# Delta heads: squares taken in the units' rounds, tail loads and residual loads moved, accumulator banks taken singly

## The reference

```
# layer 0
q, k, v, z, g, beta = project(h), with a short convolution and silu on q, k, v
o = delta_forward + delta_backward                      # [768, 8 heads, 128]
o = rmsnorm(o) * norm_g * silu(z)                       # mean of squares over the 128 of a head
y = o @ dn_w_out
x = layernorm(ALPHA * x + gt1 * y) ;  x = layernorm(ALPHA * x + gt2 * swiglu(x))   # context rows too
# layer 1
y = subln(softmax(q0 k0) v - lambda * softmax(q1 k1) v) @ da_w_out                 # 512 rows only
x = layernorm(ALPHA * x + gt1 * y) ;  x = layernorm(ALPHA * x + gt2 * swiglu(x))
```

## Time and profile before

| | us |
|---|---|
| median of 3 runs | 4401.18 (4395.31 to 4401.67) |
| profiled execution | 4397.03, its span 4395.1 |
| PE busy | 3927.8 (89% of the span) |
| DVE, ACT, POOL busy | 2124.2, 1593.9, 589.2 |
| PE idle, longest single wait in an output projection | 22.3 |

### The profile page before, as it was taken

How to read it: one execution, slowest core, us unless ns; L and a number is a source line. 1 busy time by engine, 2 the same in 40 slices (tenths; PEclk the granted TensorE clock), 3 DMA queues, 4 the chain that set the end, 5 groups by cost and what they waited for, 6 DMA issues and landing times.

```text
span 4395.1 us, 67095 instructions
## 1 busy us (share of the span) xinstructions
PE 3927.8 (89%) x28034; PEld 3252.3 (74%) x28034; DVE 2124.2 (48%) x3091; ACT 1593.9 (36%) x2560; POOL 589.2 (13%) x692
## 2 busy tenths in 40 slices
PE   6978897877999987987799988899999998899999
PEld 4866686765888775755688776677788787677887
DVE  3545454646221353266423566454655437645564
ACT  3332333333111223154222333543434335544333
POOL 0044303632000001001200000200120003100220
PEclk9988898888999999999899986899999999899999
DMA  4243433121221121102133230031233230222222
GB/s 154 76 150 123 137 94 114 34 95 48 68 68 58 53 69 67 58 10 88 56 98 96 82 77 20 22 125 49 87 98 102 86 106 31 89 96 68 96 96 86
DMA packets 248532, 355.04 MB, mean 81 GB/s; under 512 B 9299, under 2 KB 158502, under 8 KB 247846
## 3 DMA queue, kind: packets, MB, share of 16 engines
q1 hardware_dynamic: 233840, 300.49, 21.2%
q0 software_dynamic: 13840, 50.11, 3.6%
q10 hardware_dynamic: 550, 0.17, 0.0%
HBM read 336.50 MB, written 14.24 MB: 80 GB/s over the span
## 4 chain that ended last, share of the span: by engine, by line
PE 76%; DVE 11%; ACT 7%; POOL 2%; issue 2%; DMA 1%; ACTq 0%; DVEq 0%; SPq 0%; POOLq 0%
PE psum L233 20%; PE psum L235 20%; PE psum L234 20%; PE psum L230 13%; ACT arena L341 3%; PE psum L239 3%; DVE arena L264 3%; DVE arena L274 2%; POOL arena L379 2%; DVE rx L335 1%; ACT arena L345 1%; DVE arena L278 1%; DVE rw L264 1%; ACT rw L345 1%; DVE arena L270 1%
## 5 line engine op out<-in xcount | busy, mean ns | idle before, releaser
L233 PE MATMUL psum<-rx,rw 128*128 128x512 f32 (+2 forms) x2768 | 1024.9, 370 | 47.9 <-DVE rx L335 30.4
L234 PE MATMUL psum<-rx,rw 128*128 128x512 f32 (+2 forms) x2768 | 1009.3, 365 | 0.0
L235 PE MATMUL psum<-rx,rw 128*128 128x512 f32 (+2 forms) x2768 | 1008.1, 364 | 0.0
L230 PE MATMUL psum<-arena 32*32 32x32 f32 (+10 forms) x13078 | 834.2, 260 | 177.5 <-ACT arena L345 59.7
L264 DVE TENSOR_TENSOR rw<-arena,rw 128x2048 fp32r<-128x2048 f32 (+2 forms) x239 | 535.4, 2240 | 898.7 <-ACT rw L345 893.9
L230 PEld LDWEIGHTS psum<-arena 32*32 32x32 f32 (+5 forms) x13078 | 652.6, 144 | 340.7 <-issue 101.6
L345 ACT ACTIVATE rw<-arena 128x2048 fp32r<-128x2048 f32 (+2 forms) x239 | 448.1, 1875 | 847.1 <-PE psum L235 824.6
L233 PE MATMUL psum<-rw,rx 128*128 128x512 f32 (+1 forms) x1720 | 679.7, 395 | 79.7 <-DVE arena L264 40.9
L234 PE MATMUL psum<-rw,rx 128*128 128x512 f32 (+1 forms) x1720 | 673.2, 391 | 0.0
L235 PE MATMUL psum<-rw,rx 128*128 128x512 f32 (+1 forms) x1720 | 673.1, 391 | 0.0
L233 PEld LDWEIGHTS psum<-rx,rw 128*128 128x128 f32 (+1 forms) x2768 | 529.8, 191 | 146.1 <-DVE rx L335 42.7
(11 more groups left out here) (71 smaller groups left out, 2055.0 us busy)
## 6 DMA issues: line engine op xcount, KB each, us to landing
arena<-in_ffn_w_up SPq DMA_DIRECT2D x66, 1024.0 KB, 5.2
arena<-in_ada_w SPq DMA_DIRECT2D x48, 1024.0 KB, 5.2
arena<-in_ffn_w_down SPq DMA_DIRECT2D x40, 1024.0 KB, 5.0
arena<-in_ffn_w_gate SPq DMA_DIRECT2D x22, 1024.0 KB, 5.3
arena<-in_dn_w_in SPq DMA_DIRECT2D x32, 512.0 KB, 5.3
arena<-in_xa_w_kv SPq DMA_DIRECT2D x16, 1024.0 KB, 5.0
arena<-in_hgrn_w_in SPq DMA_DIRECT2D x16, 1024.0 KB, 5.5
arena<-in_da_w_in SPq DMA_DIRECT2D x12, 1024.0 KB, 5.1
```

The source lines that it names most:

```text
L230: return self.e.matmul(out, l, r, start=start, stop=stop)
L233: self.e.matmul(out, l[0], r[0], start=start, stop=False)
L234: self.e.matmul(out, l[0], r[1], start=False, stop=False)
L235: return self.e.matmul(out, l[1], r[0], start=False, stop=stop)
```

## The change

Five things.

1. The 24 squares of a group (`act_tail_square`, one for each chunk and head) are no longer made at the tail. ACT makes them during the units, one at the end of a round: the one of chunk of unit n and head h4 from round 5n + 25 + h4 on, what is left after the last round (`rest`), ahead of the meeting. Then mean, root and reciprocal are made once for all 24 columns. The transposes and gates of the tail come one round (group 0) or one step k (group 1) earlier.
2. `pool_tail_loads` stands before the meeting instead of behind it, waits for `qS` of unit 11, and for group 1 its places are those of k^ (`WK`) and of its transpose (`WK + 2 * HB`) instead of the units' memory. As `tail_first` now lies in `K.X`, the load of `x` and `ctx` (`x1`) waits for `o_lo` of head 3 and stands behind the gate rows and layer norm rows; the gate rows go to `UB`.
3. In layer 1 the rows come back into the place of v (`da_rows`, `WK + 10240`), right after the attention's last product; POOL's gain and bias (`res2`) follow that load at once, and `dve_out` reads them there (`old`) and writes `K.X`.
4. `pe_out` takes each bank just before its first matmul, not all `nt` at the start of a half.
5. The remaining loads of POOL's list in layer 1 (gate rows, layer norm rows, constants) stand behind the `res2` work.

```
@@ pe_out
     for c, (h, k0, kn) in enumerate(out_chunks(Kn)):
         if k0 == 0:
-            bs = [p.bank(tag, t, h) for t in range(nt)]
+            bs = {}
...
+            if t not in bs:
+                bs[t] = p.bank(tag, t, h)
@@ dve_out
-                    v.stt(xs, xs, ALPHA, tmp, MUL, ADD).then_inc(*v.sig((tag + "_x", t, h)))
+                    was = xs if old is None else old[:, t, h * 512:(h + 1) * 512]
+                    v.stt(xs, was, ALPHA, tmp, MUL, ADD).then_inc(*v.sig((tag + "_x", t, h)))
@@ pe_dn_proj
-        if hg and 2 <= r < 6:
-            pe_tail(p, K, 0, r - 2)
+        if hg and 1 <= r < 5:
+            pe_tail(p, K, 0, r - 1)
@@ act_dn_proj
-        if hg and r < 4:
-            act_tail_square(a, K, 0, r)
-            a.root(tail_sums(K, r), ("tail", 0, r))
+        if hg and r == 0:
+            act_tail_root(a, K, 0)
@@ dve_dn_proj
+        if hg and r == 0:
+            dve_tail_root(v, K, 0)
         if hg and r < 4:
-            dve_tail_mean(v, K, 0, r)
             dve_tail_norm(v, K, 0, r)
...
+SQUARES = [(n, h4) for n in range(12) if second_visit(n) for h4 in range(4)]
+def act_tail_square(a, K, hg, n, h4):
+    c = UNITS[n][1]
+    a.wait_ge(*K.at("o", hg, n))
+    a.act(K.mem(CO + 2016, 128), o_sum(K)[:, c, h4, :], ACT.Square, accum_out=tail_sums(K)[:, c * 4 + h4:c * 4 + h4 + 1]
+          ).then_inc(*a.sig(("tail_ss", hg)))
+def act_square_rounds(a, K, hg):
+    left = list(SQUARES)
+    def each(rnd):
+        if left and rnd >= 5 * left[0][0] + 25 + left[0][1]:
+            act_tail_square(a, K, hg, *left.pop(0))
+    def rest():
+        while left:
+            act_tail_square(a, K, hg, *left.pop(0))
+    return each, rest
...
+def dve_tail_root(v, K, hg):
+    ss, rq = tail_sums(K), norm_mem(K)[0][:, 0:24]
+    v.wait_ge(*K.at("tail_ss", hg))
+    v.tt(ss, ss, rq, MUL).then_inc(*v.sig())
     v.tt(ss, ss, rq, MUL).then_inc(*v.sig())
+    v.rstd(ss, 128.0, 1e-6, ("tail", hg))
+    v.tt(ss, ss, rq, MUL).then_inc(*v.sig())
...
 def act_last_tail(a, K):
+    act_tail_root(a, K, 1)
+    a.wait_ge(*K.at("o_ld"))
     for s in range(6):
         if s < 4:
-            act_tail_square(a, K, 1, s)
-            a.wait_ge(*K.at("o_ld"))
             act_tail_hi(a, K, s, tail_first(K, s))
-            a.root(tail_sums(K, s), ("tail", 1, s))
...
@@ pool_tail_loads
-    g.own()
     if hg:
         g.load(("o_ld",), [(tail_first(K, h4), K.o_s[h4]) for h4 in range(4)])
+    g.wait_ge(*K.at("qS", hg, 11))
     g.load(("z_ld", hg), [(tail_gate(K, hg, h4), K.z_s[hg * 4 + h4]) for h4 in range(4)])
...
@@ act_program
-        staggered([act_unit(a, K, hg, n) for n in range(12)], side)
+        each, rest = act_square_rounds(a, K, hg)
+        staggered([act_unit(a, K, hg, n) for n in range(12)], side, each)
+        rest()
@@ pool_program
+        pool_tail_loads(g, K, hg)
         g.meet(f"delta{hg}")
-        pool_tail_loads(g, K, hg)
-    x, c = (K.I[n][0].rearrange("(t p) n -> p t n", p=128) for n in ("x", "ctx"))
-    g.load(("x1",), [(K.X[:, 0:4, :], x), (K.X[:, 4:6, :], c)])
-    pool_gates(g, K, ("gate_rows", 0, 0), 0, 0, WK + 6144, 2)
+    pool_gates(g, K, ("gate_rows", 0, 0), 0, 0, UB, 2)
     pool_ln_cols(g, K)
     pool_ln_rows(g, K, ("ln_rows", 1), CO + C_ONE, "ln1", 0)
+    g.wait_ge(*K.at("o_lo", 3))
+    g.load(("x1",), [(K.X[:, 0:4, :], x), (K.X[:, 4:6, :], c)])
...
-    g.wait_ge(*K.at("daT", 7))
-    g.load(("x2",), [(K.mem(WK, 4096), K.x_s)])
+    g.load(("x2",), [(da_rows(K), K.x_s.rearrange("p (t n) -> p t n", n=1024))])
+    pool_affine(g, K, "res2", range(4), ("ln_rows", 2), WK + 7168, lambda t: ("x2",), da_rows(K))
...
-    pool_affine(g, K, "res2", range(4), ("ln_rows", 2), WK + 7168, lambda t: ("x2",))
```

More of the change, by code:

```diff
@@ L816, in act_out, with dve_out @@
             between[c]()
-def dve_out(v, K, tag, Kn, nt, src=None, gate=None, between=(), after=None, made=0, have=None, begun=0):
+def dve_out(v, K, tag, Kn, nt, src=None, gate=None, between=(), after=None, made=0, have=None, begun=0,
+            old=None):
     between, end = dict(between), len(out_chunks(Kn))
@@ L962, in pool_ln_rows, with pool_affine @@
     g.load(key, [(row, K.I[f"{which}_{n}"][i].partition_broadcast(128)) for row, n in zip(pair_of(K, base), "gb")])
-def pool_affine(g, K, tag, tiles, rows, base, ready):
+def pool_affine(g, K, tag, tiles, rows, base, ready, X):
     gain, bias = pair_of(K, base)
@@ L970, in pool_affine @@
         g.wait_ge(*K.at(*ready(t)))
-        g.tt(K.X[:, t, :], K.X[:, t, :], gain, MUL).then_inc(*g.sig())
-        g.tt(K.X[:, t, :], K.X[:, t, :], bias, ADD).then_inc(*g.sig((tag, t)))
+        g.tt(X[:, t, :], X[:, t, :], gain, MUL).then_inc(*g.sig())
+        g.tt(X[:, t, :], X[:, t, :], bias, ADD).then_inc(*g.sig((tag, t)))
 def swiglu_order(nt):
@@ L1397, in dve_dn_proj @@
             v.tile()
-        if hg and 2 <= r < 6:
-            dve_tail_gate(v, K, 0, r - 2)
+        if hg and 1 <= r < 5:
+            dve_tail_gate(v, K, 0, r - 1)
 def dve_norms(v, K, hg):
@@ L1488, in prior, with staggered @@
     return (hg, n - 2) if n >= 2 else None
-def staggered(units, side):
+def staggered(units, side, each=None):
     units, live, rnd = list(units), [], 0
@@ L1502, in staggered @@
             next(side, None)
+        if each:
+            each(rnd)
 def pe_unit(p, K, hg, n):
@@ L1801, in tail_gate, with tail_sums @@
 def tail_gate(K, hg, h4):
-    return K.mem(WK + h4 * HB + 3 * 768, 768) if hg == 0 else K.mem(UB + h4 * 768, 768)
+    return K.mem(WK + h4 * HB + 3 * 768, 768) if hg == 0 else K.mem(WK + 2 * HB + h4 * 768, 768)
 def tail_first(K, h4):
-    return K.mem(UB + HB + h4 * 768, 768)
-def tail_sums(K, h4):
-    return K.small(316, 24)[:, h4 * 6:h4 * 6 + 6]
+    return K.mem(WK + h4 * 768, 768)
+def tail_sums(K):
+    return K.small(316, 24)
 def tail_rows(K, h4):
     return o_sum(K)[:, :, h4, :]
+SQUARES = [(n, h4) for n in range(12) if second_visit(n) for h4 in range(4)]
[13 more added lines that the diff above has]
+    return each, rest
 def pe_tail(p, K, hg, h4):
@@ L1825, in pe_tail, with act_tail_root @@
         p.close("tail", hg, h4, s)
-def act_tail_square(a, K, hg, h4):
-    for c in range(6):
-        a.act(K.mem(UB + 7704, 128), o_sum(K)[:, c, h4, :], ACT.Square, accum_out=tail_sums(K, h4)[:, c:c + 1]).then_inc(
-            *a.sig(("tail_ss", hg, h4)))
-def dve_tail_mean(v, K, hg, h4):
-    ss, rq = tail_sums(K, h4), norm_mem(K)[0][:, 0:24].rearrange("p (c h) -> p c h", h=4)[:, :, h4]
-    v.wait_ge(*K.at("tail_ss", hg, h4))
+def act_tail_root(a, K, hg):
+    a.root(tail_sums(K), ("tail", hg))
+def dve_tail_root(v, K, hg):
+    ss, rq = tail_sums(K), norm_mem(K)[0][:, 0:24]
+    v.wait_ge(*K.at("tail_ss", hg))
     v.tt(ss, ss, rq, MUL).then_inc(*v.sig())
     v.tt(ss, ss, rq, MUL).then_inc(*v.sig())
-    v.ts(ss, ss, 1.0 / 128.0, 1e-6, MUL, ADD).then_inc(*v.sig(("ms", "tail", hg, h4)))
+    v.rstd(ss, 128.0, 1e-6, ("tail", hg))
+    v.tt(ss, ss, rq, MUL).then_inc(*v.sig())
 def dve_tail_norm(v, K, hg, h4):
-    ss, rq = tail_sums(K, h4), norm_mem(K)[0][:, 0:24].rearrange("p (c h) -> p c h", h=4)[:, :, h4]
-    v.wait_ge(*K.at("sd", "tail", hg, h4))
-    v.rcp(ss, ss).then_inc(*v.sig())
-    v.tt(ss, ss, rq, MUL).then_inc(*v.sig())
-    rows = tail_rows(K, h4)
+    ss, rows = tail_sums(K).rearrange("p (c h) -> p c h", h=4)[:, :, h4], tail_rows(K, h4)
     v.tt(rows, rows, bcl(ss, 128), MUL).then_inc(*v.sig(("tail_n", hg, h4)))
@@ L3972, in dve_program @@
     dve_ln_cols(v, K, "m2", 0, 0, 24, 32)
-    dve_out(v, K, "dn_out", 8, 6, gate=pair_of(K, WK + 6144), after=dve_ln_after(v, K, "ln1", t2), begun=1)
+    dve_out(v, K, "dn_out", 8, 6, gate=pair_of(K, UB), after=dve_ln_after(v, K, "ln1", t2), begun=1)
     yield "ln1"
@@ L4058, in pool_program @@
     pool_ln_rows(g, K, ("ln_rows", 2), WK + 7168, "ln2", 0)
-    g.wait_ge(*K.at("daT", 7))
-    g.load(("x2",), [(K.mem(WK, 4096), K.x_s)])
+    g.load(("x2",), [(da_rows(K), K.x_s.rearrange("p (t n) -> p t n", n=1024))])
+    pool_affine(g, K, "res2", range(4), ("ln_rows", 2), WK + 7168, lambda t: ("x2",),
+                da_rows(K))
     pool_gates(g, K, ("gate_rows", 1, 1), 1, 1, WK + 17408, 1)
@@ L4065, in pool_program @@
     g.load(("consts2",), [(K.mem(CO + 128, C_MAIN - 128), K.consts[:, 128:C_MAIN])])
-    pool_affine(g, K, "res2", range(4), ("ln_rows", 2), WK + 7168, lambda t: ("x2",))
     yield "ln3"
-    pool_affine(g, K, "res3", range(4), ("ln_rows", 3), WK + 18432, lambda t: ("m4_read", t // 2))
+    pool_affine(g, K, "res3", range(4), ("ln_rows", 3), WK + 18432, lambda t: ("m4_read", t // 2), K.X)
     yield "b1"
```

13 lines of the change are left out of this document (8 added, 5 removed).

## The result

| | before | changed |
|---|---|---|
| median of the runs, us | 4399.54 (4 runs, 4395.31 to 4401.67) | 4330.57 (4 runs, 4324.57 to 4333.30) |
| profiled execution, its time and its span | 4397.03, 4395.1 | 4329.3, 4327.5 |
| granted clock over the span | 0.932 | 0.937 |

The ratio is 0.9843, 95% interval 0.9825 to 0.9860: 69.0 us less. The forecast was 4341 (4324 to 4366), 58.5 less; it was too small by 10 us.

The account below looks back on a forecast made before the run. PE was taken as the bound: the chain that ended last lies on it for 76% of the span. Terms 11.8 + 22.1 + 7.4 + 21.8 - 3 = 60.1 off 4397.0 give 4336.9; median 4.2 above: 4341, range 4324 to 4366.

Parts of the forecast that it names:

- A: First rounds of group 1's projection: PE's waits before round 2's sums and round 4's transposes go; 11.8 us gained.
- B: Delta mixer's output projection: PE's waits for low parts and second-half banks go, but one of 1.0; 22.1 us gained.
- C: Layer 0's down projection: the 8.23 us wait for banks goes, 2.3 lost a chunk later; 7.4 us gained.
- D: Layer 1's output projection: PE's 22.31 us wait goes as residual rows load earlier; 21.8 us gained.
- E: The 33 squares moved into the units' rounds of both groups: 3 us lost, bounds 0 and 14.
- The seven squares: Step in A: seven ACT squares, 0.43 us apart, stand ahead of the meeting, so everything starts 1.4 us late.
- the 8.73: PE's wait in us before the second half of B, put down to PE taking all six banks before its first matmul.
- the lock's price: In D, DVE and POOL exclude each other on their shared port; 2 us lost for PE, between 0 and 5.
- R1: Rival: new waits (x1 late with a restart, lock 5 in D, round 4 of A) eat a fifth; 4353, chance 0.17.
- R2: Rival: each square in the rounds opens a PE wait with restart, 2.9 us, 95 in all; 4433, chance 0.04.
- R3: Rival: the bank edit brings nothing in B and C, since what follows waits as long; 4359, chance 0.06.
- R4: Rival: loads start as k, q, v are left, some 8 us before units end; B gains up to 5; 4336, chance 0.04.

Follow-up runs that it names:

- e_x_late: Changed kernel with the load of the residual rows x1 behind the operand's last low part (7), not low part 3: 4337.70 us, ratio 0.9867.
- e_allbanks: Changed kernel with the banks of an output stage taken all at once again: 4361.84 us, ratio 0.9918.
- e_best2: Kernel of e_best with DVE's weight tile in the delta output projection moved behind low part 3: 4323.80 us, ratio 0.9827.
- e_banks: Kernel before the change, with only the banks of the output stages taken one by one: 4366.05 us, ratio 0.9927.
- e_three_calls: Changed kernel, banks one by one only in delta output, layer 0's down and layer 1's output projection, all at once in other calls: 4334.96 us, ratio 0.9852.
- e_early: Changed kernel with the last tail's head and gate loads issued earlier and, in group 0, ACT's note for the meeting ahead of its last squares: 4330.54 us, ratio 0.9848.
- e_best: Kernel of e_early with head 0's high and low parts made ahead of the root: 4324.27 us, ratio 0.9836.

## Why the prediction was right, and where its sizes were off

The sum of the prediction was 60.1 us; the two traces differ by 67.6. Each term beside what its stages show, before less changed:

| term | predicted | in the traces | off by |
|---|---|---|---|
| A with its start | 11.8 | 13.9 - 1.5 = 12.4 | +0.6 |
| B with its start | 22.1 | 21.0 + 0.4 = 21.4 | -0.7 |
| C | 7.4 | 7.5 | +0.1 |
| D | 21.8 | 23.0 | +1.2 |
| E, squares in the rounds | -3 | not seen | +3.0 |
| behind D, other calls of the output function | not counted | 3.4 | +3.4 |
| all the rest, same code | 0 | -0.1 | -0.1 |

- The rest, -0.1, is luck: in these two traces the units are 4.1 us shorter, and the stretch ahead of them and those between B, C and D 4.1 longer, with what differs from trace to trace anyhow. So one pair of traces checks the single stages and not the sum.
- A. The seven squares did hold the meeting: 1.5 for the 1.4 worked out. The clock time of the first matmul (516.62, predicted 517.7) hides that, since the units ended 1.2 earlier. The waits and restarts gave 13.9 for 13.15.
- B. As predicted: the load 0.6 earlier within its chain and no more, one wait at step 3 (1.33 for 1.0), none for banks. `x1` had 6.2 us to spare and not 2 (`e_x_late`), 3.9 of them by a landing in 10.1 us for 14.0. That the 8.73 was the banks and nothing else, `e_allbanks` shows.
- C. A wait of 1.39 for L335 a chunk later where I had 2.3, and 7.5 in all in every trace that takes the banks one by one.
- D. The mechanism as predicted, the lock's price nearly: 0.7 and 2.1 at the two weight tiles, for 2 in all. Against it the waits at the end of the stage are shorter (4.8 for 7.2 in sum), which I had not counted. Of the nine traces with both edits, six stand at 52.0 to 52.7 and three at 55.1 or 55.2; in those the gain is 20 and my 21.8 was 1.7 too much. The difference begins with DVE's three operations on 16 columns ahead of the weight tile. In the changed kernel one of them took 2.4 us, in sum 2.81; in the three slower traces two of them took 2.2 to 2.3 each, in the two at 52.5 and 52.7 one did and another 0.9 to 1.2. Here they are in `e_best2`, DVE in order of time:

```profile
2012.81 4.67 DVE L264 TENSOR_TENSOR arena<-arena 128x16 f32<-128x16 f32 x3
2017.58 4.47 DVE L264 TENSOR_TENSOR rw<-arena,rw 128x2048 fp32r<-128x2048 f32 x1
```

Tile and PE behind them are 2.0 later by that, and PE's wait of 2.7 where the changed kernel has 0.67 costs clock as well. The granted clock of the 4.9 us behind each, in `e_best2` and in the changed kernel:

```profile
2022.10:2027.00 4.90, 4.89 (x14) 3.87 (x15) 4.58 (x5) 0.00 (x0) 4.90 (x7) 0.65 0.78 251
```
```profile
2031.10:2036.00 4.90, 4.85 (x21) 4.01 (x22) 4.54 (x5) 1.38 (x1) 4.82 (x2) 1.00 0.68 216
```

That costs 1.6 more; the second wait of 2.1 falls away, and the end of the stage takes 1.4 longer: 2.9 in all. In the Trainium skill, "SBUF — State Buffer", section "SBUF: two separate sides", the port goes as a whole to whoever starts first, for a whole instruction. The trace agrees: an operation on 16 columns takes 0.18 us alone (three in 0.60 before) and up to 2.4 beside one of POOL's, 2.3 to 2.7 each; and the one of POOL's that meets DVE's weight tile takes 4.3, so POOL waits as well.
- E. The step that was mis-sized: "With ACT busy less than a third I take 3 lost". Its argument spoke for nothing lost; doubling the squares cost 1.0 in the median, within the noise. The units of group 0 took 295 to 301 in the four traces without squares in the rounds and 294 to 299 in the nine with them.
- The sum. The step that failed, if only by 3.4 us, is the list of places: I looked for waits over 1.5 us near the code that changes, and the bank edit is in a function that is called ten times. Two of the waits for a bank that I left out, PE of the kernel before in order of time:

```profile
3060.55 0.47 PE L233 MATMUL psum<-rw,rx 128*128 128x512 f32 x1 [0.83 <-DVE arena L264]
...
3802.52 3.34 PE L239 MATMUL psum<-arena 128*128 128x128 f32 x16 [2.65 <-DVE arena L264]
```

The first is in the first cross attention's output projection (the second one's has its like, 0.84), the second between the halves of the last mixer's output. The three places gave 4.5, and 1.0 of other stretches went the other way. `e_banks` and `e_allbanks` moved these waits in step with the edit, and `e_three_calls` put them back alone.
- R1's condition did not come, and its restart was priced at half of what it costs (`e_x_late`). R2 is excluded, R3 too. R4's condition did not hold in the changed kernel, as it said (POOL's list). Where it is made true (`e_early`), the wait ahead of B is 3.0 shorter, and 5.9 less 0.8 in B where head 0's parts go ahead of the root too (`e_best`): the 5 us that R4 gave, in the stage; in the medians it is not shown.

What stays open: the step from 67.6 between two traces to 69.0 between the medians is within the spread of the runs. Whether D can be kept at 52 each time was not tried.

## What to carry to other kernels

Price an edit in a shared function at each of its calls, small waits too. A small wait costs its own length here (0.83 made its stretch 0.9 longer), a long one a restart on top (8.73 made B 10.8 longer). Take a buffer when the first instruction needs it and not with its whole set; and where two edits act on one wait, price them together, since here each alone left the other's wait standing (8.1 and 10.4, together 23.0). Work that was moved into an engine's idle time cost nothing that could be measured here, where the idle time is spread through the same rounds: whether that holds elsewhere can be tested by doubling it, as here.

## What the runs showed of the hardware

- Behind short waits of PE the granted clock stayed at full: 1.00 after the waits of 0.67 and 2.09 in D and of 1.33 in B, and after the one of 0.83 in the cross attention. Behind 2.66 (`e_x_late`) it was 0.50 for over 5 us, behind 2.71 (`e_best2`) 0.65 over 4.9 us, behind 8.73 (`e_allbanks`) 0.50 for 2.5 us. What PE lost beyond the wait itself was about 3, 1.6 and 2 us, so the 1.5 of the prediction is at the low end.
- A stage of large matmuls repeats to hundredths of a microsecond (C 106.87 to 106.90 in ten traces). In the units, with the same instructions, PE slips by steps of 0.9 to 1.6 us at places that differ from trace to trace, and the granted clock of the window moves with it (0.82 where the stretch took 298.8 to 300.7 us, 0.86 where it took 294.6). That sets what a single trace can tell. Why it slips is open.
- Programs that are equal around layer 1's output projection end it in 52.1 or 55.1 us, by whether one or two of DVE's three small operations wait for one of POOL's.
- The same load (1 MB of residual rows) landed in 10.1 us and not 14.0. Before, 3 MB of heads and gates were issued in the 5 us ahead of it; in the changed kernel they have landed long since, and in `e_x_late`, issued still later, it took 10.2. This was not tested alone.
